# Scores of the latent heads 1 to 7: one float32 product against three products of rounded high and low parts

## What is computed

```python
q_nope = rms_norm(q[..., :MLA_NOPE], g_mla_q_nope[l])
q_pe = rope(rms_norm(q[..., MLA_NOPE:], g_mla_q_pe[l]), positions)
k_mla = jnp.concatenate([k_nope, jnp.broadcast_to(k_pe, (B, S, MLA_HEADS, MLA_ROPE))], axis=-1)
q_mla = jnp.concatenate([q_nope, q_pe], axis=-1)
o_mla = causal_dense_attention(q_mla, k_mla, v_mla, (MLA_NOPE + MLA_ROPE) ** -0.5)
# causal_dense_attention, for each block of 128 queries:
s = jnp.einsum('bqhd,bkhd->bhqk', qi, k).astype(jnp.float32) * scale
s = jnp.where(mask, s, NEG_INF)
p = jax.nn.softmax(s, axis=-1)
```

## Time and profile before

| what | value |
| --- | --- |
| median of 3 runs | 2537.31 us (2536.9 to 2537.57) |
| the profiled execution's own time | 2535.25 us |
| its span, first to last instruction | 2533.9 us |
| mean granted TensorE clock | 0.998 |
| TensorE busy | 2508.5 us (99%) |
| VectorE busy | 1262.6 us (50%) |
| ScalarE busy | 969.5 us (38%) |
| TensorE's part of the chain that ended last | 98% |

### The profile page before, as it was taken

The page is one execution under the profiler, slowest core; times in us unless marked ns, Lnnn a source line. Parts: engine busy times, 40 slices in busy tenths (PEclk is TensorE's granted clock), DMA queues, the critical chain, the costliest instruction groups (busy, mean ns, idle before and its releaser), DMA issues.

```text
span 2533.9 us, 27943 instructions
## 1 busy us (share of the span) xinstructions
PE 2508.5 (99%) x11585; PEld 2037.8 (80%) x11585; DVE 1262.6 (50%) x1809; ACT 969.5 (38%) x1340; POOL 179.6 (7%) x186
## 2 busy tenths in 40 slices
PE   8999999999999999999999999999999999999998
PEld 5677778888888888888888888888888888888886
DVE  6777786664343333467633333333333576433333
ACT  5475554432232222347422222322222465322221
POOL 1131000000011100000011000010100000011100
PEclk9999999999999999999999999999999999999999
DMA  7434223332322222322232233222223322222231
GB/s 295 144 117 138 67 98 121 115 117 100 116 85 99 100 100 100 116 100 67 93 107 92 91 102 114 100 94 90 99 100 114 112 76 83 100 100 100 92 107 67
DMA packets 41793, 267.76 MB, mean 106 GB/s; under 512 B 5593, under 2 KB 5977, under 8 KB 12098
## 3 DMA queue, kind: packets, MB, share of 16 engines
q1 hardware_dynamic: 37824, 257.44, 29.5%
q0 software_dynamic: 2592, 7.10, 0.8%
q10 hardware_dynamic: 1250, 1.42, 0.2%
HBM read 262.78 MB, written 4.21 MB: 105 GB/s over the span
## 4 chain that ended last, share of the span: by engine, by line
PE 98%; DVE 1%; ACT 0%; DMA 0%; issue 0%; ACTq 0%
PE ps L432 30%; PE ps L434 30%; PE ps L433 30%; PE ps L1018 1%; PE ps L1054 1%; PE ps L706 1%; PE ps L663 1%; PE ps L723 1%; PE ps L677 0%; PE ps L599 0%; PE ps L1039 0%; PE ps L601 0%; PE ps L734 0%; PE ps L600 0%; PE ps L614 0%; PE ps L471 0%
## 5 line engine op out<-in xcount | busy, mean ns | idle before, releaser
L1786 DVE TENSOR_TENSOR wlo<-raw,whi 128x2048 fp32r<-128x2048 f32 x211 | 483.4, 2291 | 1033.6 <-ACT whi L1192 1033.5
L432 PE MATMUL ps<-ahi,whi 128*128 128x512 f32 x2272 | 895.7, 394 | 1.5 <-ACT tmp L1407 1.1
L434 PE MATMUL ps<-alo,whi 128*128 128x512 f32 x2272 | 885.1, 390 | 0.0
L433 PE MATMUL ps<-ahi,wlo 128*128 128x512 f32 x2272 | 884.5, 389 | 0.0
L1192 ACT ACTIVATE whi<-raw 128x2048 fp32r<-128x2048 f32 x211 | 403.8, 1914 | 865.2 <-PE ps L434 860.5
L432 PEld LDWEIGHTS ps<-ahi,whi 128*128 128x128 f32 x2272 | 426.6, 188 | 95.2 <-issue 7.8
L434 PEld LDWEIGHTS ps<-alo,whi 128*128 128x128 f32 x2272 | 426.5, 188 | 89.8
L433 PEld LDWEIGHTS ps<-ahi,wlo 128*128 128x128 f32 x2272 | 426.8, 188 | 89.2 <-issue 2.6
L432 PE MATMUL ps<-hhi,whi 128*128 128x512 f32 x1008 | 392.5, 389 | 0.0
L433 PE MATMUL ps<-hhi,wlo 128*128 128x512 f32 x1008 | 392.1, 389 | 0.0
L434 PE MATMUL ps<-hlo,whi 128*128 128x512 f32 x880 | 342.3, 389 | 0.0
(11 more groups left out here) (409 smaller groups left out, 1748.2 us busy)
## 6 DMA issues: line engine op xcount, KB each, us to landing
raw<-wstream SPq DMA_DIRECT2D x221, 1024.0 KB, 4.8
raw<-wstream SPq DMA_DIRECT2D x24, 512.0 KB, 5.1
early<-ada_in SPq DMA_DIRECT2D x8, 1024.0 KB, 20.4
strip<-bias_strips POOLq DMA_DIRECT2D x16, 256.0 KB, 3.9
x<-x_in SPq DMA_DIRECT2D x2, 1024.0 KB, 6.5
bias_strips<-bias_by_distance POOLq DMA_DIRECT2D x1, 2048.0 KB, 16.5
y_out<-x SPq DMA_DIRECT2D x3, 512.0 KB, 2.7
bd<-lru_in ACTq DMA_DIRECT2D x2, 256.0 KB, 3.3
```

The source lines that it names most:

```text
L432: pe.matmul(out, wh, rhi, start=start, stop=False)
L433: pe.matmul(out, wl, rhi, start=False, stop=False)
L434: return pe.matmul(out, wh, rlo, start=False, stop=stop)
L1786: dve.tensor_tensor(lo_of(u)[:], raw[r][:], hi_of(u)[:].bitcast(F32), ALU.subtract).then_inc(*inc("lo_dve", "lo", u))
```

## The change

`head_scores` is unchanged for head 0. For the heads 1 to 7 it issues three float32r products for each block of queries, 12 for a head in place of 4: high query x high key, low query x high key, high query x low key. The parts are made by a new function of the same name on two engines. ScalarE copies the 96x512 query and the 96x512 key of head h with rounding into `head_hi[h]`; VectorE subtracts these from the originals into `qt_lo` and `kt_lo`. TensorE now waits for the second subtraction (`k_lo`) and `top(h - 1)`; the waits for the head's parts moved to ScalarE, ahead of its copies. The new tiles lie over space that is free or no longer read at that time, which is why ScalarE also waits for the scores of head h-1 before it overwrites `head_hi`.

```diff
+        qt_lo, kt_lo = region("qt_lo", 9, [P, 8, S], F32R), region("kt_lo", 17, [P, 8, S], F32R)
+        head_hi = {h: [region(f"head_hi{h}{n}", tile, [P, S], F32R) for n, tile in enumerate((17, 9) if h == 1 else (17, 18) if h == 2 else (18, 19))] for h in range(1, 8)}
...
             def head_scores(h, *free):
                 for step in free:
                     pe.wait_ge(*at(*step))
-                pe.wait_ge(*at("head", ("kn", h // 2)))
-                if h in (0, 2):
-                    pe.wait_ge(*at("k_pe", h // 2))
-                pe.wait_ge(*at("q_pe", h))
-                if h > 0:
+                if h == 0:
+                    pe.wait_ge(*at("head", ("kn", 0)))
+                    pe.wait_ge(*at("k_pe", 0))
+                    pe.wait_ge(*at("q_pe", 0))
+                    products = ((qt[:, 0, :], kt_[:, 0, :]),)
+                else:
+                    pe.wait_ge(*at("k_lo", h))
                     pe.wait_ge(*at("top", h - 1))
+                    q_hi, k_hi = head_hi[h]
+                    products = ((q_hi[:], k_hi[:]), (qt_lo[:, h, :], k_hi[:]), (q_hi[:], kt_lo[:, h, :]))
                 for i in Q_ORDER:
                     b, off, _ = QAT[i]
-                    ins = pe.matmul(ps[:, b, off:off + P * (i + 1)], qt[0:96, h, P * i:P * (i + 1)], kt_[0:96, h, 0:P * (i + 1)], start=True, stop=True)
+                    for n, (q, k) in enumerate(products):
+                        ins = pe.matmul(ps[:, b, off:off + P * (i + 1)], q[0:96, P * i:P * (i + 1)], k[0:96, 0:P * (i + 1)], start=(n == 0), stop=(n == len(products) - 1))
...
+            def head_scored(h):
+
+                act.wait_ge(*at("scores", h - 1))
+                act.wait_ge(*at("head", ("kn", h // 2)))
+                if h == 2:
+                    act.wait_ge(*at("k_pe", 1))
+                act.wait_ge(*at("q_pe", h))
+                for n, (name, tile) in enumerate((("q", qt), ("k", kt_))):
+                    act.activation(head_hi[h][n][0:96, :], tile[0:96, h, :], ACT.Copy).then_inc(*inc("score_hi", name + "_hi", h))
...
             head_exp(0)
+            head_scored(1)
...
+                if h < 7:
+                    head_exp(h + 1)
+                if h < 6:
+                    head_scored(h + 2)
                 if h == 5:
-                    head_exp(h + 1)
                     head_seed("z", 7, EPS)
-                elif h < 7:
-                    head_exp(h + 1)
...
+            def head_scored(h):
+                for n, (name, tile, low) in enumerate((("q", qt, qt_lo), ("k", kt_, kt_lo))):
+                    dve.wait_ge(*at(name + "_hi", h))
+                    dve.tensor_tensor(low[0:96, h, :], tile[0:96, h, :], head_hi[h][n][0:96, :].bitcast(F32), ALU.subtract)\
+                        .then_inc(*inc("score_lo", name + "_lo", h))
...
             head(("kn", 3), 1)
+            head_scored(1)
             sine(("z", 1))
...
                 if h:
                     ada_acc(10 + h)
+                if h and h < 7:
+                    head_scored(h + 1)
                 if h % 2:
                     split(9 + h // 2)
```

## The result

The changed kernel takes 2550.86 us in the median (2549.53 to 2550.91), the kernel before 2537.11 (2535.67 to 2537.57) beside it. The ratio is **1.0056**, with a 95% interval of 1.0045 to 1.0068: slower by 13.75 us, where 5.9 were forecast (2543.2, range 2540.4 to 2545.2). The profiled execution took 2550.82 us. The direction was right and the size was not.

A forecast was written before the change was run, and what follows sets the result against it. TensorE, busy 99% of the span, was taken as the bound. 0.45 + 3 x 0.57 + 1.08 + 2.94 - 0.26 gave +5.9 us on 2537.31, so 2543.2 us, range 2540.4 to 2545.2.

The forecast's parts named there:

- the stall: At head 7's scores, TensorE waits for VectorE's subtractions: 2.94 us late by order of work, about 3.9 us without work.
- the clock falls during the stall: Rival: at head 7 the clock drops to 1.2 GHz, losing 3 us more, 2546 us; 7 in 100.
- TensorE's own work: Score products of a head: twelve float32r take 1.90 us against 2.16 for four float32, gaining 0.26 a head.
- ScalarE and VectorE: Making a head's parts: ScalarE's copy taken as 633 ns, VectorE's subtraction as 687 ns, the same for 96 rows.
- Head 1: Head 1's scores: TensorE waits 0.75 us for the parts and then gains 0.26, net +0.5 us (0.45 to 0.55).
- Heads 4 and 6: Their scores: subtractions ahead of `split` make the parts 0.86 us late, net +0.57 us each.
- Head 2: Head 2's scores: charged +0.57 us, the same as heads 4 and 6.
- Heads 3 and 5: Their scores: parts ready early, but the 0.26 us gain is waited away at `moved`, net 0.
- The seed: ScalarE's seed ahead of head 7, at 211.09 us: moved by 2.2 us and the copies' 1.08, starting 3.3 later.
- the gain alone: Rival: no wait on the path, seven heads gain 0.26 each, 1.8 us, giving 2535.5 us; 7 in 100.
- Only head 7 stalls: Rival: delays of heads 1 to 6 are swallowed in gaps, 3.8 us remain, 2541.1 us; 16 in 100.
- Faster: Rival: faster than accounted for, for instance narrow products without load time and head 7's wait absorbed; 4 in 100.

The follow-up runs named there:

- e9: The kernel before, unchanged, profiled once more: 2538.26 us in that execution, with both early falls of the clock.
- e11: As e8, but GpSimd makes low parts for heads 2 to 6 only, heads 1 and 7 keeping their float32 product: 2536.97 us, ratio 1.0005.
- e6: e1 with head 1 keeping its float32 product, so nothing waits for its parts: 2539.98 us, ratio 1.0013.
- e1: The changed kernel with VectorE's two subtractions for head 7 moved ahead of the root and `ada_acc`: 2540.74 us, ratio 1.0014.
- e7: The changed kernel with VectorE's subtractions for head 7 placed between the root and `ada_acc`: 2542.61 us, ratio 1.0024.
- e8: The changed kernel with head 1 in float32, GpSimd subtracting for heads 2 to 7, and ScalarE's copies at the turn's end: 2542.15 us, ratio 1.0021.
- e2: The changed kernel with ScalarE's seed of the root moved ahead of its two copies for head 7: 2546.74 us, ratio 1.004.
- e5: The changed kernel with only head 7 in three products; heads 1 to 6 keep their float32 product, without parts: 2545.9 us, ratio 1.0034.
- e4: The changed kernel with its copies, subtractions (results dropped) and waits, but scores as four float32 products as before: 2549.17 us, ratio 1.0049.
- e10: The changed kernel, unchanged, profiled once more: 2548.3 us in that execution.
- e3: The kernel before with three float32r products for heads 1 to 7 on other, ready data; no copies, subtractions or new waits: 2534.98 us, ratio 0.9993.

## Why the prediction was off, point by point

**Like with like.** e9 (before) and the profile of after have the same two early falls. Their difference is 2550.82 - 2538.26 = 12.56 us, and all but 0.2 of it is the change's (0.2 is there ahead of head 1 already, transposes at 143.66 and 143.85). The last transposes ahead of head 7's scores and the first ones behind the slow stretch, in e9:

```profile
220.48 0.38 PE L706 MATMUL ps<-const,E 128*128 128x128 f32 x2
228.30 1.03 PE L706 MATMUL ps<-const,E 128*128 128x128 f32 x8
```

And in after:

```profile
223.68 0.38 PE L713 MATMUL ps<-const,E 128*128 128x128 f32 x2
240.81 1.04 PE L713 MATMUL ps<-const,E 128*128 128x128 f32 x8
```

Ahead of the stall TensorE is 3.2 us late, 3.0 of it by the change; the stall adds 3.4 and the products give back 0.2: **6.2 us** by the order of work. At 240.81 it is 12.5 us late, so nothing is lost afterwards, and the other **6.2 us** lie between, and fit the clock: of the 13.6 us at the lower level TensorE still stood 0.8, and 12.8 us of work at half speed lose at most 6.4. Forecast were 5.9 and 0. The medians lie 13.75 apart, since that of after (2550.86) is near its profile with both early falls and that of before (2537.11) is below e9's.

**The step that failed** is the clock, which the sum put at nothing: it stood only in the rival "the clock falls during the stall", given 7 in 100 and 3 us, half of it outside the range. It cost 6.2. I had the stall (3.9 predicted, 3.36 measured) and the row of the end, where the clock fell after 3.6 us without work, and read it as if a stall had to reach that length. The prediction's last sign of being wrong, a granted clock below 1 behind 220 us, is what came. The runs show much shorter stalls with a fall behind them. All figures are from the profiled executions: the longest idle time of TensorE between 215 and 230 us, the sum of its two idle times there (the `vtok` wait, and the one at head 7's scores or behind them), the mean clock from 222 to 242, and the time at the lower level worked out from it (to within 0.2, as the mean has two digits):

| kernel | longest idle | both idle times | mean clock | at 1.2 GHz | half of that |
| --- | --- | --- | --- | --- | --- |
| e11 | 0.78 | 1.2 | 1.00 | 0 | 0 |
| e6 | 0.96 | 1.6 | 1.00 | 0 | 0 |
| e1 | 0.98 | 1.7 | 1.00 | 0 | 0 |
| e7 | 1.58 | 2.6 | 0.91 | 3.6 | 1.8 |
| e8 | 2.28 | 3.1 | 0.83 | 6.8 | 3.4 |
| e2 | 2.35 | 3.3 | 0.74 | 10.4 | 5.2 |
| e5 | 3.40 | 3.6 | 0.74 | 10.4 | 5.2 |
| e4 | 3.38 | 4.1 | 0.66 | 13.6 | 6.8 |
| after, e10 | 3.36, 3.38 | 4.4 | 0.66 | 13.6 | 6.8 |

Every profile with an idle time of 1.58 us or more had the fall, none of the three below it, and its price grew with the stall. By the longest idle time e5 is out of order; by the sum of both none is, since in e5 `vtok` is waited for 0.17 us and not 0.7 to 1.0. Which of the two counts was not tested by itself. Nothing in the trace of before excluded such falls. Given even odds, the rival would have been near the likeliest case, and priced as measured it gives 2537.3 + 6.2 + 6.2 = 2549.7. My price was half of the start-up stretch, cut to 3 without a reason for the cut. That stretch (some 10 us) was no upper bound either: 13.6 us were measured. And it rests on the lengths of products alone (one of 512 columns takes 2.08 us at 18.30, two take 1.96 at 20.68), since the windows view has the granted clock at 1.00 from 0 to 24 us.

**TensorE's own work.** Twelve products of a head take 2.00 us from the first start to the next instruction's, against 2.16 before; on the path, with the transposes ahead counted in, the gain is about 0.23 a head, forecast 0.26. Head 1 of after, in the timeline of TensorE:

```profile
145.69 0.47 PE L670 MATMUL ps<-head_hi,head_hi 96*128 96x512 f32 x1 [0.80 <-DVE kt_lo L2234]
146.00 0.39 PE L670 MATMUL ps<-head_hi,qt_lo 96*128 96x512 f32 x1
147.06 0.27 PE L670 MATMUL ps<-head_hi,qt_lo 96*128 96x128 f32 x1
147.17 0.27 PE L670 MATMUL ps<-kt_lo,head_hi 96*128 96x128 f32 x1
147.69 0.38 PE L713 MATMUL ps<-const,E 128*128 128x128 f32 x2
```

The 128-key products start 0.11 apart, as taken. The Trainium skill, "TensorE: Matmul & The Clock Gate", section "LDWEIGHTS (loading the stationary operand)", has 107 ns for the load of 128 columns; the trace agrees, with 0.11. The first product of a head takes 0.31 to the next instead of 0.23: that is the missing 0.08. The wait is not its cause, as head 5 of after (197.58, 197.90) and every head of e3, where nothing is waited for, have the same.

**ScalarE and VectorE.** Copies of 612 to 627 ns and subtractions of 679 to 687 ns, seven of each kind, close to what was taken from the earlier trace rows.

**Head 1**: wait 0.80, forecast 0.75. **Heads 4 and 6**: waits of 0.54 and 0.54; the lateness against e9 grows by 0.55 and 0.56 there, forecast 0.57 each. **Head 2** waited 0.47 in e6 and e4, but not in after, where the slow stretch near 150 us let VectorE get ahead; in after the heads 1 and 2 together cost 0.57 (the lateness goes from 0.19 to 0.76), not 1.0. **Heads 3 and 5**: no wait, and the gain is given back as said: behind head 5 the lateness falls from 1.38 to 1.13 and is 1.37 again after the next half unit.

**The seed.** The root starts at 219.35 against 215.52 in e9, +3.8 (3.6 without the 0.2 of the start); forecast 3.3. In the sum stands the copies' 1.08, which e2 confirms with 1.01. Not in the sum is a small step of VectorE that the change never touched, the scaling of head 6's maxima (128x4): it takes 1.03 us at 213.55, against 0.17 in before and e9. GpSimd has an operation from 213.28 to 214.55, and the step ends at 214.58. In e9 that operation starts at 211.86, 0.1 us behind the step; in the seven profiles in which head 6 waits the two meet, and the step takes 0.73 to 1.03 us. With 0.86 more here and 0.4 less by head 2, the root is 0.3 to 0.5 later than forecast. That the two block each other is argued from these times alone.

**`vtok`** is what I didn't see. The same two copies, and the step above, also push `head_values(6)`, for which TensorE waits 1.02 us ahead of head 6's transposes. By the order of work it adds nothing to the sum, since VectorE's chain sets the time of head 7's scores anyway: TensorE was made late a turn sooner, and the stall is shorter for it, 3.36 and not 3.9.

**The base.** The median of before hides the early falls. I saw that it stood 2.1 us above the profiled execution and left it at that; e9 shows what can be in it: 3 us between an execution with both falls and one with none.

**Rivals**: "the gain alone" is e3's kernel, about 0.7 us in the trace and not 1.8, and only without parts. "Only head 7 stalls" is near e5's mechanism, and that kernel is slower than the 3.8 by the clock (9.8 us in the medians). "Faster" has nothing in its favour.

**Open**: what decides in one execution whether the clock falls at 150 us, where the idle time is the same with and without a fall (1.1 us for `moved`, at whose end the fall lies; nine of thirteen profiles have it). At 25 us the profiles do differ: the six with the fall have an idle time of 1.40 to 1.53 us ending near 24 us, the seven without it none above 1.28. Why that wait differs from execution to execution was not looked into. Open too is how often the fall behind head 7 comes in kernels such as e7 and e8, and which of the idle times sets its length.

## What to carry to other kernels

A wait put in front of TensorE in dense work cost its length here and then one to two times as much again, where the clock fell behind it: price the fall into a forecast with a stall like these (at head 7, 1.58 us was the shortest that had one), and cut such a stall in parts (e7) or move it behind TensorE's next work (e1) before doing anything finer. An engine that is busy half of the time is not free ahead of the point at which TensorE needs it; ask what stands in its list there, and move two instructions (e1) before giving up a change. And look for the size of the prize first: here it was some 0.7 us, with fourteen copies and fourteen subtractions to pay for it.

## What the runs showed of the hardware

- The clock fell in otherwise dense work with longest gaps of 1.58, 2.28, 2.35 and 3.4 us, and stayed at 1.2 GHz for 3.6, 6.8, 10.4 and 10.4 to 13.6 us, though TensorE worked all that time but for the end of the gap (0.8 us in after). Gaps up to 0.98 us in this stretch had none behind them. Each is one profiled execution, two for after.
- The same program shows or lacks falls of 3.4 us near 25 and 150 us from one execution to the next; the two together are worth 3 us, the larger part of its spread. Near 25 us the fall goes with an idle time of 1.40 us or more, near 150 us with nothing that the profiles show.
- VectorE's operations in SBUF beside GpSimd's subtractions took 1.41 for 0.43, 1.65 for 0.75 and 4.53 for 2.46 us, and in after a step of 0.17 us took 1.03 beside a GpSimd operation that had not been beside it before. Work given to the idle GpSimd was paid for on VectorE.
